# A value layer norm split between ScalarE, a spatial mix and its bias, in a two-model fp32 kernel on one core

## The reference, cut to what matters

```python
def chunked_spatial_gating(z, ln_g, ln_b, w_s, b_s):
    u, v = jnp.split(z, 2, axis=-1)
    v = layer_norm(v, ln_g, ln_b)
    v = v.reshape(bn, s // CHUNK, CHUNK, A_HEADS, HEAD_DIM)
    w = jnp.where(causal, w_s, jnp.zeros_like(w_s))
    mixed = jnp.einsum('hts,bcshd->bcthd', w, v) + b_s.T[None, None, :, :, None]
    return u * mixed.reshape(bn, s, A_WIDTH)
```

## Time and profile before

| What | Value |
|---|---|
| median of 3 runs | 2426.64 us (2424.92 to 2430.2) |
| the profiled execution's own time | 2430.51 us |
| its span | 2428.8 us |
| PE busy | 2354.3 us, 97% |
| DVE busy | 1339.7 us, 55% |
| ACT busy | 937.3 us, 39% |
| POOL busy | 1124.9 us, 46% |
| mean granted clock of PE | 0.985 |

### The profile page before, as it was taken

The page is one execution under the profiler, slowest core; times in us unless marked ns, Lnnn a source line. Parts: engine busy times, 40 slices in busy tenths (PEclk is TensorE's granted clock), DMA queues, the critical chain, the costliest instruction groups (busy, mean ns, idle before and its releaser), DMA issues.

```text
span 2428.8 us, 33897 instructions
## 1 busy us (share of the span) xinstructions
PE 2354.3 (97%) x11781; PEld 1915.6 (79%) x11781; DVE 1339.7 (55%) x2132; ACT 937.3 (39%) x1495; POOL 1124.9 (46%) x529
## 2 busy tenths in 40 slices
PE   7988999999999999999999899999999999999998
PEld 6776778888877678888887688888888978888886
DVE  6887677673348852111157957364567473736455
ACT  3457342222335833222244453222246384322222
POOL 2336445454535634444455634434354463343443
PEclk9999999999999999999999999999999999999999
DMA  7641345554322022222222222222232202232322
GB/s 303 224 155 36 113 139 207 189 185 138 111 83 74 10 96 87 97 97 101 95 96 90 67 96 92 99 95 96 95 113 96 96 19 70 95 100 91 104 87 78
DMA packets 70095, 262.01 MB, mean 108 GB/s; under 512 B 7904, under 2 KB 8416, under 8 KB 68960
## 3 DMA queue, kind: packets, MB, share of 16 engines
q1 hardware_dynamic: 66816, 251.01, 30.2%
q10 hardware_dynamic: 3168, 9.50, 1.1%
HBM read 258.38 MB, written 2.10 MB: 107 GB/s over the span
## 4 chain that ended last, share of the span: by engine, by line
PE 82%; DVE 8%; issue 3%; DMA 2%; POOL 2%; ACT 1%; POOLq 1%; DVEq 1%; SPq 0%; ACTq 0%
PE bank L724 25%; PE bank L726 25%; PE bank L725 24%; PE bank L894 2%; PE bank L882 2%; PE bank L913 2%; DVE modraw L1924 1%; POOL w_lo L646 1%; DMA modraw<-in_blocks 1%; DVE acc L1651 1%; POOLq L712 1%; POOL prob L664 1%; DVE bank L2258 1%; DMA raw<-in_panels 1%; PE bank L826 1%
## 5 line engine op out<-in xcount | busy, mean ns | idle before, releaser
L646 POOL TENSOR_TENSOR w_lo<-raw,w_hi 128x1024 fp32r<-128x1024 f32 x378 | 945.8, 2510 | 1184.1 <-ACT w_hi L1239 1182.3
L724 PE MATMUL bank<-h_hi,w_hi 128*128 128x512 f32 x1760 | 696.5, 396 | 14.1 <-DVE h_lo L1698 7.8
L725 PE MATMUL bank<-h_lo,w_hi 128*128 128x512 f32 x1760 | 690.5, 392 | 0.0
L726 PE MATMUL bank<-h_hi,w_lo 128*128 128x512 f32 x1760 | 689.9, 392 | 0.0
L1239 ACT ACTIVATE w_hi<-raw 128x1024 fp32r<-128x1024 f32 x378 | 392.4, 1051 | 409.2 <-PE bank L726 406.4
L724 PE MATMUL bank<-g_hi,w_hi 128*128 128x512 f32 x1072 | 421.1, 393 | 0.0
L726 PE MATMUL bank<-g_hi,w_lo 128*128 128x512 f32 x1072 | 420.9, 393 | 0.0
L725 PE MATMUL bank<-g_lo,w_hi 128*128 128x512 f32 x1072 | 417.3, 389 | 0.0
L724 PEld LDWEIGHTS bank<-h_hi,w_hi 128*128 128x128 f32 x1760 | 334.0, 190 | 94.7 <-DVE h_lo L1698 8.7
L726 PEld LDWEIGHTS bank<-h_hi,w_lo 128*128 128x128 f32 x1760 | 333.7, 190 | 71.1
L725 PEld LDWEIGHTS bank<-h_lo,w_hi 128*128 128x128 f32 x1760 | 334.0, 190 | 69.3 <-issue 0.8
(11 more groups left out here) (295 smaller groups left out, 2457.1 us busy)
## 6 DMA issues: line engine op xcount, KB each, us to landing
raw<-in_panels SPq DMA_DIRECT2D x378, 512.0 KB, 3.4
modraw<-in_blocks SPq DMA_DIRECT2D x80, 512.0 KB, 5.0
first_mods<-in_first SPq DMA_DIRECT2D x4, 2048.0 KB, 22.2
x<-in_x SPq DMA_DIRECT2D x1, 2048.0 KB, 8.2
w<-in_w ACTq DMA_DIRECT2D x1, 2048.0 KB, 9.1
out<-yout ACTq DMA_DIRECT2D x8, 256.0 KB, 2.2
mask<-in_causal ACTq DMA_DIRECT2D x1, 1024.0 KB, 5.0
mask<-in_dilated ACTq DMA_DIRECT2D x1, 1024.0 KB, 6.9
```

The source lines that it names most:

```text
L646: pool.tensor_tensor(w_lo[:, slot, :], raw[:, slot, :], w_hi[:, slot, :].bitcast(F32), ALU.subtract)\
L724: pe.matmul(out, w_h, m_h, start=start, stop=False)
L725: pe.matmul(out, w_h, m_l, start=False, stop=False)
L726: return pe.matmul(out, w_l, m_h, start=False, stop=stop)
```

## The change

DVE no longer touches the values after the statistics, except for one instruction of 128x4 that makes minus mean times factor (`lnst` column 10). ACT then does four ACTIVATEs of 128x512 with that as bias and the token's factor as scale, in place in `v2t`. They stand on ACT between the copy of chunk 3 and `make_taps(P_U - 1)`.

The channel's gain is applied after the mix, in the instruction that adds the bias (now a `scalar_tensor_tensor`, the gain a per-partition scalar), since the mix is over tokens only. The channel's offset passes the mix as offset times the row sums of the masked weights. PE makes these row sums with 8 products of `ones` and `wsT` into bank 7, behind the root of the first model's last norm, and DVE adds offset times row sums to `bs` by four instructions of 128x128 behind `norm_h(3)`. For that POOL masks `wsT` earlier, after the fourth split behind the last attention. `rows` shrinks from three rows to one (768 KB to 256 KB), and `cols` grows by 8 columns.

```diff
             attention(1)
-            split_from(P_OUT1 + RING, P_AG - P_OUT1 - RING)
+            split_from(P_OUT1 + RING, 4)
             pool.wait_ge(layer2_landed, 48)
             pool.affine_select(out=wsT[:, :, :], ...).then_inc(ws_masked, 1)
-            split_from(P_AG, P_TAP + RING - P_AG)
+            split_from(P_OUT1 + RING + 4, P_TAP - P_OUT1 - 4)
...
             rstd(3)
+            pe.wait_ge(ws_masked, 1)
+            for c in range(4):
+                for b in range(2):
+                    m = pe.matmul(bank[7][HD * b:HD * b + HD, P * c:P * c + P], ones[:, 0:HD], wsT[:, 2 * c + b, :],
+                                  start=True, stop=True)
+            m.then_inc(ws_summed, 1)
             ffn(1, P_FFN1, 3)
...
             pe.wait_ge(vln_ready, 1)
-            pe.wait_ge(ws_masked, 1)
...
             act.activation(cout[:, 3, :], bank[PE_TAP_BANK][:, :], ACT.Copy).then_inc(chunk3_ready, 1)
+            act.wait_ge(vnorm_ready, 1)
+            for j in range(QB):
+                m = act.activation(v2t[:, j, :], v2t[:, j, :], ACT.Identity, bias=lnst[:, j, 10:11], scale=lnst[:, j, 9:10])
+            m.then_inc(vln_ready, 1)
             make_taps(P_U - 1)
...
             norm_h(3)
+            dve.wait_ge(ws_summed, 1)
+            for c in range(4):
+                dve.scalar_tensor_tensor(out=bs[:, c, :], in0=bank[7][:, P * c:P * c + P], scalar=col("vlnb", c),
+                                         in1=bs[:, c, :], op0=MUL, op1=ADD)
             ffn(1, P_FFN1, 3)
...
             dve.reciprocal(lnst[:, :, 9:10], lnst[:, :, 8:9])
             dve.drain()
-            for j in range(QB):
-                dve.scalar_tensor_tensor(out=v2t[:, j, :], in0=v2t[:, j, :], scalar=lnst[:, j, 6:7], in1=rows[:, 1, :],
-                                         op0=SUB, op1=MUL)
-            dve.drain()
-            for j in range(QB):
-                dve.scalar_tensor_tensor(out=v2t[:, j, :], in0=v2t[:, j, :], scalar=lnst[:, j, 9:10], in1=rows[:, 2, :],
-                                         op0=MUL, op1=ADD)
-            dve.drain()
-            dve.sem_inc(vln_ready, 1)
+            dve.scalar_tensor_tensor(out=lnst[:, :, 10:11], in0=lnst[:, :, 6:7], scalar=-1.0, in1=lnst[:, :, 9:10],
+                                     op0=MUL, op1=MUL).then_inc(vnorm_ready, 1)
...
-                dve.tensor_tensor(ysp..., bank..., bs..., ADD).then_inc(bias_added, 1)
+                dve.scalar_tensor_tensor(out=ysp..., in0=bank..., scalar=col("vlng", c), in1=bs..., op0=MUL, op1=ADD)
```

More of the change, by code:

```diff
@@ L108 @@
     ("final1", KB), ("even", KB), ("bu", 4), ("bga", 4), ("bgg", 4), ("cconv", TAPS_CONV * 4), ("cconvb", 4),
-    ("clng", 4), ("clnb", 4), ("odd", KB), ("ffn2", KB), ("ffn3", KB),
+    ("clng", 4), ("clnb", 4), ("vlng", 4), ("vlnb", 4), ("odd", KB), ("ffn2", KB), ("ffn3", KB),
     ("fw2", TAPS_FFN * 2 * FC), ("fb2", 2 * FC), ("fw3", TAPS_FFN * 2 * FC), ("fb3", 2 * FC), ("final2", KB),
@@ L246, in build @@
         wsT = v("wsT", [P, 8, P], 8)
-        rows = v("rows", [P, 3, 512], 12)
+        rows = v("rows", [P, 512], 12)
         bs = v("bs", [P, 4, P], 18)
@@ L362, in build @@
         ws_masked = sem("ws_masked")
+        ws_summed = sem("ws_summed")
+        vnorm_ready = sem("vnorm_ready")
         pad_ready = sem("pad_ready")
@@ L1508, in _ @@
             act.dma_start(wsT[:, :, :], A["wsT"]).then_inc(layer2_landed, 16)
-            act.dma_start(rows[:, :, :], A["rows"]).then_inc(layer2_landed, 16)
+            act.dma_start(rows[:, :], A["rows"]).then_inc(layer2_landed, 16)
             act.dma_start(bs[:, :, :], A["bs"]).then_inc(layer2_landed, 16)
@@ L2290, in _ @@
                     m = dve.scalar_tensor_tensor(out=v2t[:, j, at:at + 2 * P], in0=tokens_of(p, j // 2)[:, j % 2, :],
-                                                 scalar=both_inverse[:, j:j + 1], in1=rows[:, 0, at:at + 2 * P],
+                                                 scalar=both_inverse[:, j:j + 1], in1=rows[:, at:at + 2 * P],
                                                  op0=MUL, op1=ADD)
@@ L2334, in _ @@
                 undrained.clear()
-                dve.tensor_tensor(ysp[:, c % 2, :].rearrange("p (j t) -> p j t", j=QB),
-                                  bank[(P_U + c) % RING][:, :].rearrange("p (j t) -> p j t", j=QB),
-                                  bs[:, c:c + 1, :].broadcast_to((P, QB, P)), ADD).then_inc(bias_added, 1)
+                dve.scalar_tensor_tensor(out=ysp[:, c % 2, :].rearrange("p (j t) -> p j t", j=QB),
+                                         in0=bank[(P_U + c) % RING][:, :].rearrange("p (j t) -> p j t", j=QB),
+                                         scalar=col("vlng", c), in1=bs[:, c:c + 1, :].broadcast_to((P, QB, P)),
+                                         op0=MUL, op1=ADD).then_inc(bias_added, 1)
                 conv_taps(1, (0, 2, 3) if left[3] else (1,))
@@ L2501, in laid_out @@
         "cconvb": c(f["even_conv_b_2"]), "clng": c(f["even_conv_ln_g_2"]), "clnb": c(f["even_conv_ln_b_2"]),
+        "vlng": c(f["even_v_ln_g_2"]), "vlnb": c(f["even_v_ln_b_2"]),
         "odd": c(f["odd_norm_g_2"]), "ffn2": c(f["ffn_norm_g_2"][0]), "ffn3": c(f["ffn_norm_g_2"][1]),
@@ L2524, in laid_out @@
     out["wsT"] = f["even_w_s_2"][0].transpose(2, 0, 1)
-    rows = np.stack([b_in[512:1024], f["even_v_ln_g_2"][0], f["even_v_ln_b_2"][0]])
-    out["rows"] = np.broadcast_to(rows, (P, 3, 512))
+    out["rows"] = np.broadcast_to(b_in[512:1024], (P, 512))
     bs = f["even_b_s_2"][0].reshape(4, 2, 1, P)
```

## The result

| What | Before | The change |
|---|---|---|
| median | 2427.73 us (4 runs) | 2442.36 us (4 runs, 2434.36 to 2445.02) |
| the profiled execution's own time | 2430.51 us | 2434.36 us |
| mean granted clock of PE | 0.985 | 0.989 |

The change is **slower**, ratio 1.0049 with an interval of 1.0035 to 1.0063, so 8.5 to 15.3 us where +2.7 was forecast; 2442.36 lies outside the range. The profiled execution is the fastest of the four. It stood 6.5 us ahead of before when the statistics began (1348.76 against 1355.27), of which some 5 us arose in the first 270 us, where the change has no instruction of its own. So the two spans understate the loss, and stages are compared by their own lengths. Ratios leave disturbed runs out, which are two of a_gold's twelve (2591.77 and 4298.3 us, at a lower granted clock; the other ten have a median of 2433.3).

A forecast was written before the change was run, and what follows sets the result against it. The end of tap 30, which PE waits for, was taken as the bound. Tap 30 at +2.7 us and row sums at 0, on 2426.6, gave 2429.3 us; range 2423.6 to 2432.4, "same" at chance 0.80.

The forecast's parts named there:

- What bounds the kernel: At the value norm, PE waits for DVE's last convolution taps; the stage's end is tap 30 of chunk 1.
- Part 1: DVE at the value norm loses eight instructions, 14.6 us, and would reach tap 27 4.0 us earlier.
- Part 2: ACT's four passes ahead of the scaled taps take 2.6 us; the scaled taps start 5.3 us later.
- Part 3: POOL's chain of adds and splits shortens to 19.1 us; its last add ends at 1384.05 instead of 1380.90.
- Part 4: POOL's two splits hold DVE's product with u and tap 28; tap 30 ends 2.7 us later.
- rival (b): Any DVE instruction slows POOL, so its last add ends at 1387.2, tap 30 +5.8: 2432.4 us; chance 0.12.
- Rival (a): POOL's last add comes by 1381 and PE's gap almost closes: -6.5 us, or 2420.1 us; chance 0.08.
- PE's gap ahead of the last mean: PE's idle time ahead of the last mean should be near 8 us instead of 3.7.
- Part 5: Row sums on PE fit in its idle 2.59 us behind the root's spread; taken as 0, bounds +0.3 and -1.6.
- My bound of -1.6: The row sums behind the root's spread might bring PE's clock back sooner, gaining up to 1.6 us.
- The clock behind the gap: PE restarts at half clock behind the longer gap; 1 us allowed either way for when the clock returns.
- Everything behind follows tap 30 as before: All work behind tap 30 was taken to shift with it, by +2.7 us, with PE restarting at half clock as before.

The follow-up runs named there:

- a_gold: The change whole, with the region of g_hi and g_lo put back to its old place, 146624; 2434.15 us against 2428.74, ratio 1.0012.
- Experiment 7: The run a_taps: the change with ACT's four passes put behind the scaled taps; 2438.65 us, ratio 1.0040.
- Experiment 8: The run a_defer: the change with g at 146624 and POOL's last two splits behind the last tap; 2437.59 us against 2429.4.
- Experiment 1: The run b_g64: the kernel before, with g's region 64 bytes higher, at 146688; 2439.79 us against 2428.74, ratio 1.0045.
- Experiment 6: The run w64: the kernel before, with weights w_hi and w_lo 64 bytes higher, g and h unmoved; 2448.77 us against 2431.01, ratio 1.0074.
- both: The change with g's region at 146560 and ACT's four passes behind the scaled taps; 2421.01 us against 2430.47, ratio 0.9960.
- both_late: The kernel both, with POOL's last split waiting until DVE has centred the convolution; 2419.65 us against 2430.47, ratio 0.9961.
- w64: The kernel before, with weights w_hi and w_lo 64 bytes higher and g and h unmoved; 2448.77 us against 2431.01, ratio 1.0074.
- b_gh: The kernel before, with g's region at 146560, the same offset modulo 256 as the weights; 2422.70 us against 2430.47, ratio 0.9970.
- b_g64: The kernel before, with g's region 64 bytes higher, at 146688; 2439.79 us against 2428.74, ratio 1.0045.
- b_g384: The kernel before, with g's region at 146816, offset 128 modulo 256 as the weights have; one run, 2427.0 us against 2429.4.
- all64: The kernel before, with every SBUF tile 64 bytes higher, distances kept; one run, 2430.71 us against 2429.4.
- a_taps: The change, g at its new place, with ACT's four passes put behind the scaled taps of panels P_U-1 and P_U; 2438.65 us, ratio 1.0040.
- a_defer: The change with g at 146624 and POOL's last two splits waiting for the last tap of chunk 1; one run, 2437.59 us against 2429.4.
- b_g0: The kernel before, with g's region at 146432, offset 0 modulo 256; one run, 2441.77 us against 2429.4.
- a_gh: The change whole, with g's region at 146560, the weights' offset modulo 256; 2423.29 us, ratio 0.9978 of before.

## Why the prediction was wrong, point by point

**What bounds the kernel.** Right: the stage's end is the end of tap 30, and moving it moved what follows.

**Parts 1 to 4.** Right, to 0.3 us in every event of the table above. The four passes stood 0.71 us apart from start to start, not 0.65, inside the bounds of 0.60 and 0.75; the next scaled tap began 2.84 us behind the first of them (1357.85 - 1355.01), not 2.6. By the Trainium skill ("ScalarE: Activation LUTs", "What ACT_TABLE_LOAD costs"), where each per-partition operand adds about 93 ns, it was to be 0.2 to 0.4 us more than my 2.6; it was 0.24. POOL's adds read 1.27 to 1.30 without DVE's value instructions, so rival (b) fell. Rival (a) fell with the last add at +28.87. Experiments 7 and 8 show the two links apart: the delay of ACT's taps and the hold by the splits. The holding agrees with the Trainium skill ("SBUF — State Buffer", "Who interferes with whom": a DVE instruction with two SBUF inputs contends with a GpSimd instruction that reads SBUF).

PE's gap ahead of the last mean was "near 8 us" in the prediction and 9.39 in the row. I had kept the end of the mix where it was; without DVE's delays PE was done with the mix and the means earlier, so it began to wait earlier. That moves no end.

**Part 5.** The row sums are hidden. PE at the root's spread, beside the earlier trace rows:

```profile
895.84 1.55 PE L828 MATMUL bank<-ident,root 128*128 128x128 f32 x8 [1.62 <-DVE root L1670]
897.32 1.98 PE L1106 MATMUL bank<-wsT,ones 128*64 128x128 f32 x16
899.98 0.50 PE L726 MATMUL bank<-h_hi,w_hi 128*128 128x512 f32 x1 [0.68 <-DVE h_lo L1709]
```

They are done 1.98 us behind their start, at 899.30; then the first product waits 0.68 us for DVE's `h_lo`, at +4.1 us from the spread's start, as before (905.09 - 900.98 in the earlier trace rows). My bound of -1.6 for an earlier return of the clock came once: a fixed product further on (the 101st that reads `w_hi`) stands 38.28 us behind the spread's start in this execution and 39.80 in before. In the six other kernels with row sums it stands at 39.78 to 39.82, so the row sums don't bring it by themselves, and 0 was the right choice. The 3.2 us at half speed that I took from the earlier trace rows stand in no row of it; the trace of before has them (the first eight products start from 905.09 to 908.24).

**The clock behind the gap.** I allowed 1 us either way. In the profiled execution of the change 0.96 of the 2.74 us were left at the rounding of panel 206 (66.88 us against 65.92 behind the statistics). PE worked 3.9 us at half clock behind the gap, where before it worked 5.1, and it had no second such stretch behind the squares, where before had one of 2.7 us. In a_gold, with the same stage (38.70 us), the second stretch had 3.1 us, and 3.19 us were left. So two profiles of one stage lie 2.2 us apart, more than the 2 us that my allowance spans from end to end.

**The step that failed is the sum.** "Everything behind follows tap 30 as before" priced every panel of the program as unchanged, and the parts listed the edits by what they compute. The growth of `cols` by 8 columns, which stood in the description of the change, got no term at all; it was read as 4 KB more in SBUF, not as a shift of all the tiles behind it. It was worth 10.9 us (7.0 to 14.8), four times the sum of all terms that I did work out. The range missed for the same reason: its bounds came from the terms I had, and the rival on the slow side was a larger size of one of them. The trace of before held a hint: products of `h` and of `g`, of the same shapes and types, followed each other at 227 and at 229 ns, and I never compared the two operands.

The Trainium skill points the other way here. "SBUF — State Buffer", "Who interferes with whom", gives PE two independent read ports, one for the moving operand and one for the weight load, and says that PE never waits on anyone. By that rule a shift by 64 bytes costs nothing. Experiments 1 and 6 contradict its use for speed: the pace hangs on how the tiles of these two reads lie to each other. Whether it is the two reads that meet, and where, was not tested.

## What to carry to other kernels

Whoever adds a constant should ask what it moves: compare the addresses of all large tiles before and after, and the pace of the commonest instruction operand by operand, ahead of any account of the edit itself. Here the moving operand and the weights at the same offset modulo 256 bytes were worth 7.3 us of 2430 for free, more than the change's whole idea. And a stage of several engines is won by its order: the same four passes end it 3.7 us later when they stand ahead of the scaled taps than when they stand behind them.

The best versions are both and both_late: 2421.01 and 2419.65 us, 0.4% below before. Of that, 7.3 us are the offset's; about 2 us are left for the change with its passes moved, which the intervals don't tell from none.

## What the runs showed of the hardware that was not expected

- With an fp32r moving operand of 128x512 and weights of 128x128, products follow each other at 226.7, 228.9 or 233.3 ns, by the distance of the two tiles modulo 256 (0, 64, and 128 or 192). The length of the record tells less: 394 to 395 ns at 233.3, but for `g_lo` 389 at 228.9 and, in w64, 389 at 226.7.
- Behind the 32 narrow products of the squares, a second stretch at half clock came in some profiled executions (2.7 us long in before, 3.1 in a_gold, 3.2 in w64, 3.4 in b_gh, b_g64, b_g384 and all64, 3.5 in a_taps, 4.3 in a_defer, 4.9 in both_late, 5.2 in b_g0) and in others not at all (the change, a_gh, both). Before, b_gh, b_g64, b_g384, all64 and b_g0 do the same instructions in this stage with `h` at the same pace, and tap 30 ends 35.9 us behind the start of the statistics in each; yet panel 206 is rounded 65.6 to 67.5 us behind it. So the stage's edits don't decide it alone. Each kernel has one profile, and what does decide it stays open. By estimate it is worth up to 2.6 us, as much as the stage's terms.
- Two splits of POOL back to back hold two instructions of DVE one after the other (2.68 and 2.83 us), and lose 0.9 us themselves: 5.58 us for both, where the earlier trace rows has 4.70.
